# Output norm of a gated-delta layer: from one pass after the token loop to a piece per 128-token tile inside it

## What is computed

```python
def mixer_b(h, conv_buf, s0, w_in, conv_w, a_log, dt_bias, norm_w, w_out):
    ...   # proj = h @ w_in; conv and silu give c; z, beta and g come from proj as well
    q = l2norm(c[..., :H_B * DK_B].reshape(B, T, H_B, DK_B)) * (DK_B ** -0.5)
    k = l2norm(c[..., H_B * DK_B:2 * H_B * DK_B].reshape(B, T, H_B, DK_B))
    ...
    o, s_new = gated_delta_chunked(q, k, v, g, beta, s0)      # 8 heads of 128, chunks of 64 tokens
    o = rmsnorm(o, norm_w) * jax.nn.silu(z)                   # the output norm and the gate
    y = o.reshape(B, T, H_B * DV_B).astype(h.dtype) @ w_out
```

## Time and profile before

| what | value |
|---|---|
| median of 3 runs | 3141.02 us (3138.91 to 3149.06) |
| the profiled execution: its own time | 3138.51 us |
| its span in the trace | 3136.7 us |
| PE busy | 2947.4 us, 94% of the span |
| DVE busy | 1402.7 us, 45% |
| ACT busy | 933.4 us, 30% |
| POOL busy | 615.9 us, 20% |
| TensorE clock, mean | 0.94 of full |

### The profile page before, as it was taken

One profiled execution on the slowest core, in us unless ns is written; L12 is line 12 of the kernel. 1 busy time (PEld: TensorE's weight loads), 2 busy tenths in 40 slices (PEclk: granted clock), 3 DMA queues, 4 the chain that ended last, 5 costly groups with the idle time before them and its releaser, 6 DMA issues.

```text
span 3136.7 us, 55290 instructions
## 1 busy us (share of the span) xinstructions
PE 2947.4 (94%) x24181; PEld 2805.5 (89%) x24181; DVE 1402.7 (45%) x1904; ACT 933.4 (30%) x1634; POOL 615.9 (20%) x518
## 2 busy tenths in 40 slices
PE   7999799999999899989999975999999997999998
PEld 7996499999999888879999975999999973999998
DVE  4552343344677433344344347344365533444432
ACT  5554222222333411122222212222235543222222
POOL 0001141222310111014122233122230002322213
PEclk9998799999999978669999987999999988999999
DMA  3235433433323100223333321433332355243342
GB/s 109 73 91 175 125 91 126 129 118 122 107 73 82 28 2 2 68 65 92 128 123 123 123 85 54 132 123 123 119 115 68 83 160 154 75 128 124 116 128 101
DMA packets 440935, 318.48 MB, mean 102 GB/s; under 512 B 17181, under 2 KB 427470, under 8 KB 438359
## 3 DMA queue, kind: packets, MB, share of 16 engines
q1 hardware_dynamic: 430967, 277.19, 29.2%
q0 software_dynamic: 9728, 37.75, 3.9%
HBM read 299.62 MB, written 71.68 MB: 118 GB/s over the span
## 4 chain that ended last, share of the span: by engine, by line
PE 86%; DVE 6%; ACT 4%; issue 2%; DMA 2%; SPq 1%; POOL 0%; ACTq 0%; DVEq 0%; POOLq 0%
PE acc L210 67%; PE acc L939 2%; PE misc L926 1%; PE misc L883 1%; PE misc L1628 1%; PE misc L1526 1%; PE misc L1639 1%; DMA s_kv<-cache_a_kv 1%; PE acc L1666 1%; PE acc L1659 1%; PE acc L1721 1%; ACT a_sw L1063 1%; PE misc L829 1%; ACT a_p L1019 1%; PE acc L1681 1%
## 5 line engine op out<-in xcount | busy, mean ns | idle before, releaser
L210 PE MATMUL acc<-act_hi,w_hi 128*128 128x272 f32 x3856 | 814.9, 293 | 21.3 <-DVE act_lo L260 14.2
L210 PE MATMUL acc<-act_lo,w_hi 128*128 128x272 f32 x3856 | 800.7, 289 | 0.0
L210 PE MATMUL acc<-act_hi,w_lo 128*128 128x272 f32 x3856 | 800.1, 289 | 0.0
L195 DVE TENSOR_TENSOR w_lo<-w_raw,w_hi 128x1024 fp32r<-128x1024 f32 (+1 forms) x367 | 582.9, 1588 | 314.1 <-ACT w_hi L188 312.7
L210 PEld LDWEIGHTS acc<-act_hi,w_hi 128*128 128x128 f32 x3856 | 606.3, 189 | 28.6 <-issue 14.5
L210 PEld LDWEIGHTS acc<-act_lo,w_hi 128*128 128x128 f32 x3856 | 608.0, 189 | 0.0
L188 ACT ACTIVATE w_hi<-w_raw 128x1024 fp32r<-128x1024 f32 (+1 forms) x367 | 388.0, 1057 | 737.8 <-PE acc L210 676.0
L210 PEld LDWEIGHTS acc<-act_hi,w_lo 128*128 128x128 f32 x3856 | 607.2, 189 | 0.0
L210 PE MATMUL acc<-h_hi,w_hi 128*128 128x272 f32 x2048 | 425.6, 289 | 0.0
L210 PE MATMUL acc<-h_lo,w_hi 128*128 128x272 f32 x2048 | 422.4, 287 | 0.0
L210 PE MATMUL acc<-h_hi,w_lo 128*128 128x272 f32 x2048 | 422.0, 287 | 0.0
(11 more groups left out here) (361 smaller groups left out, 2623.3 us busy)
## 6 DMA issues: line engine op xcount, KB each, us to landing
w_raw<-mlp_w SPq DMA_DIRECT2D x256, 512.0 KB, 3.9
new_a_kv_s<-cache_a_kv SPq DMA_DIRECT2D x128, 381.0 KB, 4.5
s_kv<-cache_a_kv POOLq DMA_DIRECT2D x40, 768.0 KB, 6.2
w_raw<-a_w_in SPq DMA_DIRECT2D x54, 512.0 KB, 4.1
w_raw<-b_w_in SPq DMA_DIRECT2D x32, 512.0 KB, 4.1
w_raw<-a_w_out SPq DMA_DIRECT2D x16, 576.0 KB, 4.1
s_kv<-cache_a_kv POOLq DMA_DIRECT2D x32, 192.0 KB, 4.0
new_a_kv_s<-cache_a_kv SPq DMA_DIRECT2D x16, 372.0 KB, 4.6
```

The costliest lines, as they stand in the source:

```text
L195: nc.vector.tensor_tensor(w_lo[:, t.slot, 0:t.kt, :], w_raw[:, t.raw, 0:t.kt, :], w_hi[:, t.slot, 0:t.kt, :].bitcast(F32), ALU.subtract).t ...
L210: last = nc.tensor.matmul(acc[:, t.first % 2, s, 0:HALF], w[:, t.slot, k, :], a[:, k, s * HALF:(s + 1) * HALF], start=(k == 0 and i == 0), ...
```

## The change

The norm is cut into five pieces, one for each tile. For tile j:

- ACT squares q, scaled, before the outputs overwrite it (`q_squares`, after `copy_w` of tile j) and squares the outputs (`out_squares`, after level 4's copy in tile j+1); DVE adds the two (`add_squares`, after level 4 of tile j+1).
- PE multiplies ones by the sum (`out_sums`, two matmuls of 512 columns, in tile j+1 between the last `below` and `old_weights`), which leaves the sum on all 128 partitions.
- ACT takes the root of it (`out_root`, after `copy_w` of tile j+1; 128 x 1024 numbers), DVE the reciprocal in place and one product of gate, weight and factor into `b_z` (`normed`, after level 2 of tile j+2). POOL multiplies gate and output (`gated`).
- Tile 3's pieces stand at the start of the samples and after h = 3, tile 2's `normed` after h = 1, and the samples' own piece (128 x 256 numbers) at the end.

After that only copies stand ahead of `b_out`: `act_hi` on ACT and `act_lo` on DVE. The sums with one output column, the spreading matmuls, `b_rq2` and the factor arithmetic are gone. The new buffers lie in slots 2 and 3 of `w_hi` and `w_lo`, which hold no weights in the loop. The load of the convolution state counts on the same semaphore as the small constants, so PE's first setup transpose waits for it too.

```diff
+        work = {}
+        with ExitStack() as place:
+            for name in ("ow", "oq"):
+                work[f"b_{name}"] = place.enter_context(nc.sbuf_tensor(f"b_{name}", [P, 8, P], F32))
+            work["b_rs"] = place.enter_context(nc.sbuf_tensor("b_rs", [P, 8, P], F32))
+            for name in ("ows", "oqs", "rss"):
+                work[f"b_{name}"] = place.enter_context(nc.sbuf_tensor(f"b_{name}", [P, 8, 32], F32))
...
-                sp.dma_start(b_state, aps["state_b_conv"][0].rearrange("b j c -> (b j) c")).then_inc(b_clanded, 16)
+                sp.dma_start(b_state, aps["state_b_conv"][0].rearrange("b j c -> (b j) c")).then_inc(b_landed, 16)
...
+                def gated(j):
+                    tc = tcols(j)
+                    pool.wait_ge(b_oc, 2 * (j + 1) if j < QT else 2 * QT + HB_)
+                    nc.gpsimd.tensor_tensor(b_z[:, :, tc], b_z[:, :, tc], b_qkv[:, 0:HB_, tc], ALU.mult).then_inc(b_zo, 1)
...
                                                 b_lvl[0:w, k, 0:wd].unsqueeze(1).to_broadcast([w, HB_, wd]), ALU.mult).then_inc(b_m, 1)
+                    if 1 <= i < QT:
+                        gated(i - 1)
...
-                pool.wait_ge(b_oc, 2 * QT + HB_)
-                for h in range(HB_):
-                    nc.gpsimd.tensor_tensor(b_z[:, h, :], b_z[:, h, :], b_qkv[:, h, :], ALU.mult).then_inc(b_zo, 1)
+                gated(QT - 1)
+                gated(QT)
...
+                def out_sums(j, bank):
+                    w = width(j)
+                    pe.wait_ge(b_oadd, j + 1)
+                    for hb in range(2):
+                        last = nc.tensor.matmul(bank[hb][:, 0:4 * w], ones[:, :], b_ow[j][:, 4 * hb:4 * hb + 4, 0:w], start=True, stop=True)
+                    last.then_inc(b_os, 1)
+
...
                     pe.wait_ge(b_kv, i + 1)
+                    if i >= 1:
+                        pe.wait_ge(b_rt, i)
                     for hb in range(2):
...
+                    if 1 <= i < QT:
+                        pe.wait_ge(b_ex, 3 * (i + 2))
+                        out_sums(i - 1, [acc[:, 1, hb, :] for hb in range(2)])
                     old_weights(i)
...
                 old_state(0)
+                out_sums(QT - 1, [misc[2], misc[3]])
...
                     pe.wait_ge(b_vm, h + 1)
+                    if h == 1:
+                        pe.wait_ge(b_rt, QT)
...
+                out_sums(QT, [acc[:, 0, hb, :] for hb in range(2)])
                 pe.wait_ge(b_sd, HB_)
-                for h in range(HB_):
-                    pe.wait_ge(b_osqd, h + 1)
-                    sums(b_osq[:, h % 2, :], 0, misc[2], h).then_inc(b_os, 1)
...
-                    for i in range(QT + 1):
-                        w = width(i)
-                        last = nc.tensor.matmul(acc[:, h % 2, i // QT, (i % QT) * P:(i % QT) * P + w],
-                                                b_rn[0:w, i, HB_ + h:HB_ + h + 1].to_broadcast([w, P]), ident[0:w, 0:w], start=True, stop=True)
-                    last.then_inc(b_obc, 1)
-                pe.wait_ge(b_on, HB_)
...
+                def q_squares(j):
+                    w = width(j)
+                    if 1 <= j < QT:
+                        act.wait_ge(b_os, j)
+                    nc.scalar.activation(b_ow[j][:, :, 0:w], b_qkv[:, 0:HB_, tcols(j)], ACT.Square, scale=Q_EPS)
+
+                def out_squares(j):
+                    w = width(j)
+                    act.wait_ge(b_oc, 2 * (j + 1) if j < QT else 2 * QT + HB_)
+                    if 1 <= j < QT:
+                        act.wait_ge(b_oadd, j)
+                    nc.scalar.activation(b_oq[j][:, :, 0:w], b_qkv[:, 0:HB_, tcols(j)], ACT.Square).then_inc(b_osqd, 1)
+
+                def out_root(j, bank):
+                    w = width(j)
+                    act.wait_ge(b_os, j + 1)
+                    if 1 <= j < QT:
+                        act.wait_ge(b_on, j)
+                    for hb in range(2):
+                        last = nc.scalar.activation(b_rs[j][:, 4 * hb:4 * hb + 4, 0:w], bank[hb][:, 0:4 * w].rearrange("p (h n) -> p h n", h=4),
+                                                    ACT.Sqrt, scale=1.0 / P, bias=eps_o[:, 0:1])
+                    last.then_inc(b_rt, 1)
...
                         copy_Z(i, 4)
+                        if i >= 1:
+                            out_squares(i - 1)
                         exp_tokens(i + 1)
                         copy_Z(i, 5)
                     copy_w(i)
+                    if 1 <= i < QT:
+                        out_root(i - 1, [acc[:, 1, hb, :] for hb in range(2)])
+                    q_squares(i)
                 copy_o(QT - 1, 1)
+                out_squares(QT - 1)
...
-                act.wait_ge(b_oc, 2 * QT + HB_)
-                act.wait_ge(b_pout, 16)
+                    if h == 0:
+                        out_root(QT - 1, [misc[2], misc[3]])
+                out_squares(QT)
+                out_root(QT, [acc[:, 0, hb, :] for hb in range(2)])
                 act.wait_ge(b_su, HB_)
+                act.wait_ge(b_on, QT + 1)
                 for h in range(HB_):
-                    if h >= 2:
-                        act.wait_ge(b_os, h - 1)
-                    nc.scalar.activation(b_osq[:, h % 2, :], b_qkv[:, h, :], ACT.Square).then_inc(b_osqd, 1)
-                act.wait_ge(b_gate_dve, 8)
-                nc.scalar.activation(b_rn[:, :, HB_:], b_rn[:, :, HB_:], ACT.Sqrt, scale=1.0 / P, bias=eps_l2[:, 0:1]).then_inc(b_gate_act, 1)
-                for h in range(HB_):
-                    act.wait_ge(b_on, h + 1)
-                    nc.scalar.activation(act_hi[:, h, :], b_h32[:, h % 2, :], ACT.Copy).then_inc(b_ohi, 1)
+                    nc.scalar.activation(act_hi[:, h, :], b_z[:, h, :], ACT.Copy).then_inc(b_ohi, 1)
...
+                def add_squares(j):
+                    w = width(j)
+                    dve.wait_ge(b_osqd, j + 1)
+                    nc.vector.tensor_tensor(b_ow[j][:, :, 0:w], b_ow[j][:, :, 0:w], b_oq[j][:, :, 0:w], ALU.add).then_inc(b_oadd, 1)
+
+                def normed(j):
+                    w, tc = width(j), tcols(j)
+                    rs = b_rs[j][:, :, 0:w]
+                    dve.wait_ge(b_rt, j + 1)
+                    chain(dve, nc.vector.reciprocal(rs, rs))
+                    dve.wait_ge(b_zo, j + 1)
+                    nc.vector.scalar_tensor_tensor(b_z[:, :, tc], b_z[:, :, tc], nw, rs, ALU.mult, ALU.mult).then_inc(b_on, 1)
...
                         level(i, 2)
+                        if i >= 2:
+                            normed(i - 2)
                         log_pairs(i + 1)
                         left_keys(i + 1)
                         level(i, 3)
...
                         level(i, 4)
+                        if i >= 1:
+                            add_squares(i - 1)
                         decayed_q(i + 1)
...
                 new_state(QT - 1, 1)
+                add_squares(QT - 1)
...
                     if h + 2 < HB_:
                         own(h + 2)
+                    if h in (1, 3):
+                        normed(QT - 2 + h // 2)
                 state_out(HB_ - 1)
-                dve.wait_ge(b_os, HB_)
-                for i in range(QT + 1):
-                    w = width(i)
-                    last = nc.vector.tensor_tensor(b_rn[0:w, i, HB_:], misc[2][0:w, 16 * i:16 * i + HB_], b_rq2[0:w, i, :], ALU.mult)
...
-                chain(dve, nc.vector.reciprocal(b_rn[:, :, HB_:], b_rn[:, :, HB_:]))
-                nc.vector.tensor_tensor(b_rn[:, :, HB_:], b_rn[:, :, HB_:], b_rn[:, :, 0:HB_], ALU.mult).then_inc(b_gate_dve, 1)
+                add_squares(QT)
+                normed(QT)
                 for h in range(HB_):
...
-                    nc.vector.scalar_tensor_tensor(o32[:, 0:SEQ], b_z[:, h, 0:SEQ], nw, acc[:, h % 2, 0, :], ALU.mult, ALU.mult)
-                    nc.vector.scalar_tensor_tensor(o32[:, SEQ:TOK], b_z[:, h, SEQ:TOK], nw, acc[:, h % 2, 1, 0:NS], ALU.mult, ALU.mult).then_inc(b_on, 1)
                     dve.wait_ge(b_ohi, h + 1)
-                    nc.vector.tensor_tensor(act_lo[:, h, :], o32, act_hi[:, h, :].bitcast(F32), ALU.subtract).then_inc(b_olo, 1)
+                    nc.vector.tensor_tensor(act_lo[:, h, :], b_z[:, h, :], act_hi[:, h, :].bitcast(F32), ALU.subtract).then_inc(b_olo, 1)
```

More of the change, by code:

```diff
@@ L99, in build_step @@
         w_raw = sb("w_raw", [P, RAW, KMAX, P])
+        work = {}
+        with ExitStack() as place:
+            place.enter_context(nc.sbuf_tensor("w_hi_head", [P, 2, KMAX, P], F32))
+            for name in ("ow", "oq"):
+                work[f"b_{name}"] = place.enter_context(nc.sbuf_tensor(f"b_{name}", [P, 8, P], F32))
+            place.enter_context(nc.sbuf_tensor("w_hi_tail", [P, 256], F32))
+            place.enter_context(nc.sbuf_tensor("w_lo_head", [P, 2, KMAX, P], F32))
+            work["b_rs"] = place.enter_context(nc.sbuf_tensor("b_rs", [P, 8, P], F32))
+            for name in ("ows", "oqs", "rss"):
```

(27 more changed lines are left out.)

14 lines of the change are left out of this document (1 added, 13 removed).

## The result

The changed kernel takes 3137.34 us against 3144.96 us for the kernel before on the same chips (medians of 20 runs each): a ratio of 0.9978, 95% interval 0.9967 to 0.9988, or about 7 us less. The profiled execution took 3132.38 us, its span 3130.6 us (before: 3138.51 and 3136.7). The forecast was 3142 us and no difference that can be told; the gain is small, but it lies outside what chance leaves. It is also the remainder of terms of some 20 to 30 us each, and that is where the lesson is.

A forecast was written before the change was run, and what follows sets the result against it. The old norm's 39.25 us tail stood alone; in the loop PE mostly ended waits itself, with little slack for DVE's absence. -31.0 + 10.9 + 4.7 + 5.6 + 8.0 + 0.2 + 2.5 = +0.9: 3142 us, range 3133 to 3152.

The forecast's parts named there:

- Tail, -31.0: Between last state product and output projection: the old norm's 39.25 us shrink to 8.2, a gain of 31.0 us.
- The reciprocal, 6.5 us each: On DVE, four times: 1024 columns take 6.5 us, by a line through reciprocals of 5, 24 and 40 columns.
- The rivals with 1.21 and 8.6 us: Wide reciprocal on DVE: as cheap as a plain pass (3126 us), or a third steeper (3151 us); chance 0.05 each.
- `out_sums` in tiles 1 to 3: +4.7 us: PE's sums ahead of the old weights stick out of a 1.5 us gap by 0.35 or 2.15 us; total +4.7.
- the products with ones keep the clock up: Rival: full array work in PE's gap keeps the following stretch at full clock, some 5 us in two tiles; chance 0.12.
- `normed` in tiles 2 and 3: +10.9: DVE, away 7.8 us ahead of level 3's update, delays PE at level 4 by 5.7 and 5.2 us.
- Clock: +2.5: After the four stalls PE runs part of level 4 at half clock; half of one level taken, +2.5 us.
- the stalls cost their clock too: Rival: a stretch at half clock follows each of four stalls, 12 us instead of 2.5, so 3151; chance 0.18.
- The prediction's own sign of being wrong: It falls if DVE's absences don't reach PE, or PE loses its clock for longer than one level after each.
- `normed` after heads 1 and 3: +8.0: In the samples DVE, away 7.8 us, makes the next mask late: 5.4 us, then 2.7 or 5.4; bounds 7 to 10.8.
- Start of the samples, +5.6: `add_squares` of tile 3 ahead of `own(0)` +1.85, standing still beside POOL about +1.05, `out_sums` without a gap 2.7 us.
- Costed at nothing: ACT's squares and roots and POOL's `gated` in the loop run within idle time; without that cover, each under 1 us a tile.

The follow-up runs named there:

- run 1: The kernel before plus two unread products with ones (128 x 512 each) ahead of the old weights in tiles 1 to 3: 3126.32 us, ratio 0.9946.
- run 6: The changed kernel with the sums of squares of tiles 0 to 2 and their roots moved behind the next tile's first values and their copy: 3155.28 us.
- run 8: The kernel before plus 32 unread products of 64 x 64 by 64 columns ahead of the old weights in tiles 1 to 3: 3128.42 us.
- Run 3: The changed kernel without the reciprocal, multiplying by the root itself: 3107.03 us, ratio 0.9884.
- Runs 4: The changed kernel with tile 3's root in a buffer of its own: 3131.28 us, ratio 0.9960.
- run 7: The changed kernel with logarithm and exponent on ScalarE replacing root and reciprocal, and tile 3's root in its own buffer: 3101.44 us, ratio 0.9864.
- runs 3 to 7: Five variants of the changed kernel; the fifth experiment, among them, put logarithm and exponent on ScalarE in place of root and reciprocal: 3112.01 us.
- run 9: The kernel before plus one unread product with ones (two records of 512 columns) ahead of the old weights in tiles 1 to 3: 3123.42 us.

## Why the prediction was wrong

By its own steps, each with what was measured:

- **Tail, -31.0: right.** 8.4 us in place of 8.2.
- **The reciprocal, 6.5 us each: right,** and so was the step from three small sizes to one 25 times as wide. The rivals with 1.21 and 8.6 us are out.
- **"`out_sums` in tiles 1 to 3: +4.7 us": this step failed, and with its sign.** I let 0.35 or 2.15 us stick out of a gap, which they did (some 0.4 in tile 2, 1.8 in tile 3), and took the clock of the neighbours as given, which was the error. The same products alone make the later part of the loop 13.7 us shorter and the kernel 17.9 us faster (run 1), and their place is worth 17.9 us (run 6). The forecast had this as a rival, "the products with ones keep the clock up", for some 10 us and a chance of 0.12; its mechanism was right but for the full array (run 8), and its size too small. For the gain to show at all this rival had to hold.
- **"`normed` in tiles 2 and 3: +10.9": right in the main, 9.4 of added idle time. "Clock: +2.5": this step failed too, by its size.** Run 3 saves 21.7 us in these two tiles, so the clock behind the stalls is worth some 12.3 us. That is the size, 12, of the other rival, "the stalls cost their clock too" (which had half of it in the samples), and it held as well. The prediction's own sign of being wrong, clock lost for longer than one level, is there in tile 3: half clock for 18 us.
- **"`normed` after heads 1 and 3: +8.0": mis-sized, with its place missed.** First to last state product grew by 15.1 us. I counted VectorE's queue and the slack of the masks, and not that tile 3's root waits for tile 2's product (`b_on`) and a state product for the root (`b_rt`): 10.12 us at head 1, where 5.4 stood at head 2, and then 3.58 at head 4, where 2.7 stood. Runs 4 and 7 show it.
- **Start of the samples, +5.6.** TensorE's idle time grew from 1.67 to 4.66 us, by 3.0, forecast 2.9; `add_squares` took 2.39 us beside POOL's 2.35, against 1.21 alone. The sums took 1.98, forecast 2.7. The stretch as a whole grew by only 1.4 us, since the samples' old weights (3.62 us at half before, 1.97 now) and part of the work behind them ran at full clock.
- **Costed at nothing: right.** In tile 2 no wait of TensorE is put down to the squares, to a root or to POOL's `gated`; the one to ScalarE is `b_Z`'s old 0.69.

So two rivals of opposite sign came true at once: against the sum's own terms, and by the traces, the sums of squares brought 18.4 us more (-13.7 for +4.7) and the clock behind the stalls cost 9.8 more, beside 7.1 in the samples. Put in, the terms -30.8 (tail), +9.4, +12.3, -13.7, +1.4 and +15.1 give -6.3. The table shows -8.8; the other 2.5 is the first part of the loop (97.7 against 100.2), which no other kernel with the change repeats (100 to 101 us in runs 3 to 7), so I take it for chance. The forecast lay 4.7 us above the median only because these errors largely cancel: that is luck. I had treated the two as exclusive cases, each with a chance of its own; they were separate effects, and each was to be added with its own expectation.

Two sums of the prediction don't come out as written, and nothing rests on either: the bounds as given add up to 3133 and 3153 (it says 3152), and a cheap reciprocal would have cut the delays after heads 1 and 3 to near 0.1 us each, not 1.4.

That the change is worth about 22 us once these effects are out can be seen by run 9 (before, gap filled: 3123.42) against run 7 (changed, gap filled, no reciprocal: 3101.44): 31 us of tail less the rest of the new work.

What stays open: why in the kernel before the clock stays at half until 1230 although TensorE works without pause from 1215.89, when in run 1 it comes back within 3 us of work that joins on to the last. Why the stretch at half begins ahead of tile 0's old weights in some executions and behind them in others of the same code (3.68 and 2.00 us). And why the clock also falls where no pause is seen: in the kernel before, 1285 to 1292 was granted 0.97 and 1292 to 1300 ran at half (values in 3.67 us), and in run 9 1180 to 1190 was granted 0.66 with TensorE busy throughout. So pauses aren't the whole account of the clock here; what is shown is what filling this one does.
